# Running decay sums as rows: one broadcast transfer per head in place of four turns on TensorE

## The chip, the cores and the metric

The kernel runs on one NeuronCore of a Trainium2 chip. The metric is device time in microseconds for one execution of the whole program. The engines that matter here: TensorE (PE, matmuls and turns by the identity), its weight load (PEld), VectorE (DVE), ScalarE (ACT), GpSimd (POOL) and SyncE (SP), which issues the DMAs.

## The reference, cut to what matters

Two layers of a hybrid block (a gated delta rule over 8 heads, sliding-window attention, gates, an MLP), then one block with a state-space branch and a pooling branch. Sequence 512, model width 1024, everything in float32. The change touches the delta rule alone, in both layers. There, per head:

```python
g = jnp.cumsum(g, axis=-1)                       # running sum of the log decay, within a chunk
diff = g[..., :, None] - g[..., None, :]
decay = jnp.where(causal, jnp.exp(jnp.where(causal, diff, 0.0)), 0.0)
L = jnp.where(strict, jnp.einsum('bhnid,bhnjd->bhnij', kb, k) * decay, 0.0)
a_intra = jnp.einsum('bhnid,bhnjd->bhnij', q, k) * decay
q_dec = q * jnp.exp(g)[..., None]
```

The kernel works with chunks of 128 positions (4 per head), not 64. It needs the running sums `g` twice: as a column (one number per partition) and as a row (the same 128 numbers of a chunk on every partition), because `diff` has one index on the partitions and one along them, and because `q` is stored with its channels on the partitions, so that `exp(g)` must stand as a row to scale it.

## The kernel before, in words

**Products.** Activations are stored turned, channels on partitions, as [128, 8, 512]. Each weight tile of 512 KB is loaded into one of three buffers `raw` by SP (`load_weights`, lines 882 to 886, which waits until the tile three before it has been split), split into a high part by ScalarE (line 899) and a low part by GpSimd (line 906), and used in 24 matmuls of 128x512 (`products`, lines 933 to 935: high by high, high by low, low by high). An output tile is scaled out of PSUM by VectorE (line 1693).

**The order.** Every engine runs a written list. A planner, `ordered` (line 277), takes chains of stages, the needs between chains, the engine of each stage and its cost in microseconds, and always places the stage that can start first; `layer_order` (line 407) gives it the chains of one layer, and each engine's function walks through the result and does the stages that are its own. SP's list is made of weight loads (and some transfers of the third block); it waits in order like any other. Within a chain, a stage waits for a semaphore that counts the finished stages of the chain (`G.before`, `D.before`).

**The gates, chain G** (once per layer). TensorE turns the gates' projection, VectorE and ScalarE make the log decay `gg` (128 positions by 4 chunks by 8 heads), and stage "cumsum" multiplies it on TensorE by a triangle of ones and by ones (lines 1819 and 1820), into bank 0 of `psD`. "copyc" (line 1500, VectorE) copies the sums to `gcl`; "diff", "exps" and "nbeg" make three exponentials and a negation from them.

**The heads, chain D** (8 per layer). Stages in order: square, sums, qscale, turnk, ksum, root, copyk, turnv, recip, dscale, copyv, rows, diff, exps, qdec, gramk, maskk, first, minus, gramq, maskq. All that TensorE makes here goes to bank 0 of `psD`, one stage after the other. The stages near the change are these:
- "rows" (line 1834, TensorE): for each of the 4 chunks it takes the column of sums of this head, repeated along 128 columns, and turns it, so that the sums stand as a row on all partitions.
- "diff" (line 1522, VectorE): 4 instructions, rows minus column, then the minimum with a mask; the result goes to `DT`.
- "exps" (lines 1348 and 1349, ScalarE): the exponential of the rows, from PSUM into `rna` (which is the buffer `rstdp`; the trace calls it so), and that of `DT` in place.
- "qdec" (line 1272, GpSimd): q times `rna`.

After D a head goes through chain A (the inverse of the triangular matrix, many small matmuls and masks) and chain B (the scan over chunks), while the planner mixes the weight products of later tiles in between.

Of the kernel before, what the change touches and what calls it, by code (L numbers as in the profile page):

```python
# [14 lines left out]
P = 128  # L15
# [174 lines left out]
def e_stages(tile):  # L190
# [3 lines left out]
    if kind == "f2":  # L194
# [7 lines left out]
            "cumsum", "copyc", "diff", "exps", "nbeg"]  # L202

D_STAGES = ["square", "sums", "qscale", "turnk", "ksum", "root", "copyk", "turnv", "recip", "dscale", "copyv", "rows", "diff", "exps",
# [30 lines left out]
N_STAGES = ["highs", "adds"]  # L235
R_STAGES = ["cast", "angle"] + [f"{s}{i}" for s in "sc" for i in range(6)] + ["sin", "sign"]
# [85 lines left out]
for _engine, _kind, _stages in [  # L322
        ("pe", "G", "turn cumsum"), ("act", "G", "tanh abs expn ln expa exps"),
        ("pe", "D", "sums rows gramk gramq turnk turnv"), ("act", "D", "square ksum root exps copyk copyv"), ("pool", "D", "qdec"),
        ("pe", "A", "p q turn plast qlast"), ("act", "A", "copy copylast"),
        ("pe", "B", "v o r kv turno"), ("act", "B", "copyv osq square root high"), ("pool", "B", "low"),
        ("pe", "C", "score turn pv"), ("act", "C", "exp copy high"),
        ("pe", "E", "dupk turnv"), ("act", "E", "tap3 tanh copyk copyv high square"), ("pool", "E", "low"),
        ("act", "N", "highs"), ("vector", "N", "adds"), ("act", "R", "sin"), ("act", "M", "square high"), ("pool", "M", "low"),
        ("act", "Z", "dt mag sines kcopy"), ("pe", "Z", "kmm"), ("dma", "Z", " ".join(Z_DMA)),  # L330
        ("sp", "SU", "uout uin"), ("dma", "SU", "ulanded landed"), ("sp", "SY", "yout yin"), ("dma", "SY", "ylanded landed"),
        ("act", "SY", "gelu high"), ("pe", "S", "input output"), ("act", "S", "copyy"),
        ("act", "BA", "high"), ("pool", "BA", "low")]:
    for _s in _stages.split():
        LAYER_ENGINES[_kind, _s] = _engine


def micros(e):

    kind, j, s = e  # L340
    if kind == "mm":
        return 5.12 / PARTS
    if kind == "split_high":
        return 1.1
    if kind == "split_low":
# [8 lines left out]
    special = {("N", "highs"): 2.5, ("N", "adds"): 3.0, ("A", "update"): 0.45, ("A", "turn"): 0.6, ("A", "p"): 1.1, ("A", "q"): 1.1, ("A", "plast"): 0.6, ("A", "qlast"): 0.6,  # L354
# [16 lines left out]
    return special.get((kind, name), LENGTH[engine_of(e)])  # L371
# [35 lines left out]
def layer_order(layer):  # L407
# [11 lines left out]
    def needs(e):  # L419
# [64 lines left out]
        if kind == "Z" and s == "dt":  # L484
            out.append(e_last(("f1", KT - 1)))
        if kind == "G" and s == "turn":
            out.append(e_last(("ab", 0)))
        if kind == "D":
            if s == "square":
                out.append(e_last(("v", j)))  # L490
            if s == "copyk" and TAKEN[j] is not None:
                out.append(("B", TAKEN[j], "o"))
            if s == "rows" and j == 0:
                out.append(last("G", 0))
            if s == "maskk" and j >= 3:
                out.append(last("A", GROUP_OF[j - 3]))
# [19 lines left out]
    chains += [[("C", t, s) for t in range(o, SWQ, 2) for s in C_STAGES] for o in range(2)]  # L516
    chains.insert(0, [("N", i, s) for i in range(2) for s in N_STAGES])
# [150 lines left out]
def build(nc, xT, pos, consts, gain0, params, weights, params2, smallbc, uD, yD, matsD, lagsD, outT):  # L668

    with ExitStack() as ctx:  # L670
# [3 lines left out]
        def sem(name):  # L674
            return ctx.enter_context(nc.semaphore(name))
# [63 lines left out]
        ab = U1  # L739
        rna = rstdp  # L740
# [168 lines left out]
        def part(layer, earlier):  # L909
            names = ("tile_stage", "gate_stage", "gram_stage", "inverse_stage", "scan_even", "scan_odd", "window_even", "window_odd", "mlp_even", "mlp_odd",  # L910
                     "coef_stage", "x_ready", "sq_done", "h_high", "h_low", "ssq_done", "root_done", "rstd_ready", "x_scaled", "post_col", "pre_col", "pre_row",
                     "pre_sum", "sq_added", "post_sum", "coef_in", "sum_done", "post_root", "post_ready", "out_done", "setup", "out_ready", "state_stage", "y_stage",
                     "branch_even", "branch_odd", "mats_out", "mats_even", "mats_odd", "u_out", "u_even", "u_odd", "y_out", "y_in")
# [3 lines left out]
             branch_even, branch_odd, mats_out, mats_even, mats_odd, u_out, u_even, u_odd, y_out, y_in) = [sem(f"{n}{layer}") for n in names]  # L917
# [336 lines left out]
            if layer < DEPTH:  # L1254
                def run_sync(sp):
                    if layer == 0:
                        start_sync(sp)
                    for kind, j, s in L_ORDERS[layer]:
                        if kind == "load":
                            load_weights(sp, NL * layer + j)  # L1260
                        elif kind == "Z" and s.rstrip("0123") in Z_DMA:
                            coefficient_transfers(sp, s)

# [30 lines left out]
                def run_scalar(act):  # L1294
                    for kind, j, s in L_ORDERS[layer]:
# [37 lines left out]
                        elif kind == "D" and s in ("square", "ksum", "root", "exps", "copyk", "copyv"):  # L1333
# [13 lines left out]
                            elif s == "exps":  # L1347
                                act.activation(rna[:, :], psD[:, 0, :], ACT.Exp)
# [121 lines left out]
                def run_vector(v):  # L1470
                    for kind, j, s in L_ORDERS[layer]:
# [5 lines left out]
                        elif kind == "G":  # L1477
                            if s not in ("copy", "beta", "addb", "max", "plus1", "sp", "g", "copyc", "diff", "nbeg"):
                                continue
# [19 lines left out]
                            elif s == "copyc":  # L1499
                                ins = v.tensor_copy(gcl, psD[:, 0, 0:64])  # L1500
                            elif s == "diff":
# [4 lines left out]
                        elif kind == "D" and s in ("qscale", "recip", "dscale", "diff", "maskk", "maskq", "first", "minus"):  # L1506
# [233 lines left out]
                def run_tensor(pe):  # L1740
# [3 lines left out]
                    for kind, j, s in L_ORDERS[layer]:  # L1744
# [65 lines left out]
                        elif kind == "G" and s in ("turn", "cumsum"):  # L1810
# [5 lines left out]
                            else:  # L1816
# [3 lines left out]
                                ins = pe.matmul(psD[:, 0, 32:64], k_("ones"), gg, start=True, stop=True)  # L1820
                            ins.then_inc(gate_stage, 1)
                        elif kind == "D" and s in ("sums", "rows", "gramk", "gramq", "turnk", "turnv"):
# [3 lines left out]
                            if s == "rows" and h == 0:  # L1826
                                pe.wait_ge(gate_stage, G.end(0))
                            for c in range(CH):
                                i, cc = c * HEADS + h, slice(c * P, (c + 1) * P)
# [552 lines left out]
```

## Time and profile before

| | us |
|---|---|
| median of 3 runs | 2522.82 (2521.14 to 2523.16) |
| the profiled execution | 2522.34 |
| its span in the trace | 2520.6 |
| TensorE busy | 2421.3 (96%) |
| VectorE busy | 1256.3 (50%) |
| GpSimd busy | 1153.6 (46%) |
| ScalarE busy | 1057.5 (42%) |

Numbers of the sections ahead and below come from the profiled execution. "Busy" of TensorE counts the time in which at least one matmul is under way. Matmuls overlap: each of 128x512 is shown with some 390 ns, while they start 230 ns apart, so what a group of them takes is read from the starts, not from the durations. `L1834` is line 1834 of the kernel.

### The profile page before, as it was taken

The page shows a single profiled execution, that of the slowest core. Times are in us where ns is not written, and L with a number is a line of the kernel's source. Part 1 is how long each engine was busy: PE and PEld are TensorE (multiplying, and loading weights), DVE is VectorE, ACT ScalarE, POOL GpSimd, SP SyncE. Part 2 cuts the span into 40 slices and gives each one's busy share as a digit, 9 for nine tenths or more (in the row PEclk, how much of TensorE's full clock was granted, in tenths as well). Part 3 has the DMA queues.
Part 4 walks back from the last instruction along what each step waited for, and adds up shares of the span by engine and source line. Part 5 has one row for each costly group of instructions (what it writes and reads, how often), then busy time and mean ns, then how long its engine had stood idle before and what let it go on. Part 6 is the DMA issues. An engine that isn't in the chain of part 4 may idle for free.

```text
span 2520.6 us, 35035 instructions
## 1 busy us (share of the span) xinstructions
PE 2421.3 (96%) x13972; PEld 1924.9 (76%) x13972; DVE 1256.3 (50%) x2172; ACT 1057.5 (42%) x2254; POOL 1153.6 (46%) x848
## 2 busy tenths in 40 slices
PE   7999999999999999988999999999999999799998
PEld 5777777777778888766878777787777788677886
DVE  4767654673341111266667446633485511566453
ACT  5565643543343323345566434443533332313342
POOL 4323323334666555543323233356665564433464
PEclk9999999999999999989999999999999999878999
DMA  4211112122223233311111122223234332362232
GB/s 138 67 51 51 51 43 68 59 76 76 92 76 100 92 94 99 101 59 51 58 44 60 43 68 67 68 84 110 66 111 122 121 98 93 99 185 85 93 99 75
DMA packets 76514, 207.47 MB, mean 82 GB/s; under 512 B 16704, under 2 KB 27712, under 8 KB 75840
## 3 DMA queue, kind: packets, MB, share of 16 engines
q1 hardware_dynamic: 76352, 205.24, 25.9%
q8 instruction: 110, 1.80, 0.3%
q14 instruction: 52, 0.43, 0.1%
HBM read 194.72 MB, written 10.49 MB: 81 GB/s over the span
## 4 chain that ended last, share of the span: by engine, by line
PE 81%; DVE 9%; ACT 4%; POOL 2%; issue 2%; DMA 1%; SPq 0%; DVEq 0%; ACTq 0%; POOLq 0%
PE ps L933 23%; PE ps L935 21%; PE ps L934 21%; PE ps L1855 2%; PE ps L1859 2%; PE ps L1908 1%; PE ps L1920 1%; PE ps L1836 1%; POOL wL L906 1%; ACT wH L899 1%; PE ps L1914 1%; ACT prob L1404 1%; DVE ctw L1143 1%; DVE ctmp L1143 1%; PE ps L1885 1%
## 5 line engine op out<-in xcount | busy, mean ns | idle before, releaser
L906 POOL TENSOR_TENSOR wL<-raw,wH 128x512 fp32r<-128x512 f32 x660 | 901.7, 1388 | 1143.7 <-ACT wH L899 1143.4
L899 ACT ACTIVATE wH<-raw 128x512 fp32r<-128x512 f32 x660 | 379.7, 624 | 769.5 <-PE ps L935 766.1
L933 PE MATMUL ps<-hH,wH 128*128 128x512 f32 x1592 | 667.5, 419 | 11.0 <-DVE tmp L1693 8.8
L935 PE MATMUL ps<-hH,wL 128*128 128x512 f32 x1592 | 633.4, 398 | 0.0
L934 PE MATMUL ps<-hL,wH 128*128 128x512 f32 x1592 | 631.2, 396 | 0.0
L933 PEld LDWEIGHTS ps<-hH,wH 128*128 128x128 f32 x1592 | 303.7, 191 | 82.8 <-issue 22.7
L935 PEld LDWEIGHTS ps<-hH,wL 128*128 128x128 f32 x1592 | 303.4, 191 | 67.8
L934 PEld LDWEIGHTS ps<-hL,wH 128*128 128x128 f32 x1592 | 304.9, 191 | 54.9 <-issue 0.7
L933 PE MATMUL ps<-OH,wH 128*128 128x512 f32 x576 | 230.8, 401 | 4.9 <-DVE acc L1722 1.8
L935 PE MATMUL ps<-OH,wL 128*128 128x512 f32 x576 | 227.8, 396 | 0.0
L934 PE MATMUL ps<-OL,wH 128*128 128x512 f32 x576 | 227.8, 395 | 0.0
L933 PE MATMUL ps<-SH,wH 128*128 128x512 f32 x436 | 172.6, 396 | 0.0
L935 PE MATMUL ps<-SH,wL 128*128 128x512 f32 x436 | 172.5, 396 | 0.0
L934 PE MATMUL ps<-SL,wH 128*128 128x512 f32 x436 | 172.4, 395 | 0.0
L933 PEld LDWEIGHTS ps<-OH,wH 128*128 128x128 f32 x576 | 108.2, 188 | 36.7 <-issue 9.2
L1724 DVE TENSOR_TENSOR acc<-acc,ps 128x512 f32<-128x512 f32 x48 | 33.0, 687 | 202.0 <-PE ps L935 202.0
L935 PEld LDWEIGHTS ps<-OH,wL 128*128 128x128 f32 x576 | 108.2, 188 | 26.1
L934 PEld LDWEIGHTS ps<-OL,wH 128*128 128x128 f32 x576 | 108.3, 188 | 24.8
L933 PEld LDWEIGHTS ps<-SH,wH 128*128 128x128 f32 x436 | 81.9, 188 | 20.2 <-issue 0.4
L934 PEld LDWEIGHTS ps<-SL,wH 128*128 128x128 f32 x436 | 81.9, 188 | 19.8
L935 PEld LDWEIGHTS ps<-SH,wL 128*128 128x128 f32 x436 | 81.9, 188 | 19.7
L1404 ACT ACTIVATE prob<-prob,small 128x256 f32<-128x256 f32 (+1 forms) x128 | 59.9, 469 | 61.6 <-DVE small L1640 61.6
(405 smaller groups left out, 3461.8 us busy)
## 6 DMA issues: line engine op xcount, KB each, us to landing
raw<-w SPq DMA_DIRECT2D x345, 512.0 KB, 3.5
mats<-matsD SPq DMA_DIRECT2D x4, 1408.0 KB, 6.6
x<-xT SPq DMA_DIRECT2D x8, 256.0 KB, 5.8
matsD<-Cd SPq DMA_DIRECT2D x8, 256.0 KB, 2.7
matsD<-wide SPq DMA_DIRECT2D x4, 512.0 KB, 3.6
mats<-lagsD SPq DMA_DIRECT2D x32, 64.0 KB, 6.4
outT<-acc SPq DMA_DIRECT2D x8, 256.0 KB, 2.2
matsD<-tab SPq DMA_DIRECT2D x8, 128.0 KB, 1.9
```

The lines of the kernel that those rows point to most:

```text
L899: act.activation(weights_at(slot)[0][:, k, :], raw[:, n % RAW, k, :], ACT.Copy).then_inc(high_done, 1)
L906: pool.tensor_tensor(low[:, k, :], raw[:, n % RAW, k, :], high[:, k, :].bitcast(F32), ALU.subtract).then_inc(low_done, 1)
L933: pe.matmul(out, wh, rH[:, t, :], start=(t == 0), stop=False)
L934: pe.matmul(out, wh, rL[:, t, :], start=False, stop=False)
L935: mm = pe.matmul(out, wl, rH[:, t, :], start=False, stop=(t == depth - 1))
L1143: return v.tensor_tensor(o, a, b, ALU.mult)
L1404: act.activation(prob[:, i, a:], prob[:, i, a:], ACT.Exp, bias=nm4[:, i:i + 1], accum_out=den[:, i:i + 1])
L1724: ins = v.tensor_tensor(acc[:, i % 8, :], acc[:, i % 8, :], b, ALU.add)
L1836: ins = pe.matmul(psD[:, 0, cc], k[:, cc], (k if s == "gramk" else q)[:, cc], start=True, stop=True)
L1855: ins = pe.matmul(psA[b, 0, cc], lt[b, c, b], Xi[b, i, :], start=True, stop=True)
L1859: ins = pe.matmul(second_half(psA[b, 0, cc], n), Pm[b, i, :], second_half(xb[b, i, :], n), start=True, stop=True)
L1885: ins = pe.matmul(psS[e], XT[SLOT[h]][:, c, :], vb[SLOT[h]][:, 0, :] if c == 0 else rr, start=True, stop=True)
```

## The change

The 4 turns of each head go. In their place the gates' chain computes the sums once more in turned form, with `gg` as the weights and the triangle as the moving operand: 32 partitions (chunk and head) by 128 positions. A new stage "copyr" copies them to SBUF (`gclT`, 32 x 128, in a tile of the scan that is not yet in use). SP writes them to DRAM in 4 transfers, one per chunk, so that each head's 512 sums lie in one row of `yD` (a DRAM tensor of the third block). For each head SP reads that row with a broadcast over 128 partitions into `rna`. "diff" takes its rows from `rna`, and "exps" works in place there. The reads and writes are a new chain "GR" for the planner (its stages "outlanded" and "landed" stand for the landing of a transfer). The first "sums" now waits for "copyr", and the wait for the end of the gates moves from "rows" of head 0 on TensorE to "diff" of head 0 on VectorE. Semaphores that a block does not use are no longer made.

```diff
 G_STAGES = [...
-            "cumsum", "copyc", "diff", "exps", "nbeg"]
+            "cumsum", "copyc", "copyr", "diff", "exps", "nbeg"]
-D_STAGES = [..., "dscale", "copyv", "rows", "diff", "exps",
+D_STAGES = [..., "dscale", "copyv", "diff", "exps",
...
+ROWS = [(-1, "out"), (-1, "outlanded")] + [(h, s) for h in range(HEADS) for s in ("in", "landed")]
...
# the planner's costs, in its microseconds
+    special = {("GR", "out"): 1.2, ("GR", "in"): 0.4, ("GR", "outlanded"): 3.0, ("GR", "landed"): 3.5, ...
-               ("D", "rows"): 0.45,
...
# the planner's needs
+        if kind == "GR" and s == "out":
+            out.append(("G", 0, "copyr"))
+        if kind == "GR" and s == "in" and j:
+            out.append(("D", j - 1, "qdec"))
...
+            if (j, s) == (0, "sums"):
+                out.append(("G", 0, "copyr"))
+            if (j, s) == (0, "copyk"):
+                out.append(("G", 0, "exps"))
-            if s == "rows" and j == 0:
-                out.append(last("G", 0))
+            if s == "diff":
+                out.append(("GR", j, "landed"))
+                if j == 0:
+                    out.append(last("G", 0))
...
+        gclT = osqs[0][0:CH * HEADS, 0:P]
...
# SP
+                        elif kind == "GR" and s == "out":
+                            sp.wait_ge(gate_stage, G.before(0, "copyr") + 1)
+                            for c in range(CH):
+                                sp.dma_start(yD[layer, 0:HEADS, c * P:(c + 1) * P], gclT[c * HEADS:(c + 1) * HEADS, :]).then_inc(rows_out, 16)
+                        elif kind == "GR" and s == "in":
+                            if j == 0:
+                                sp.wait_ge(rows_out, 16 * CH)
+                            else:
+                                sp.wait_ge(gram_stage, D.before(j - 1, "qdec") + 1)
+                            sp.dma_start(rna[:, :], yD[layer, j:j + 1, :].to_broadcast([P, SEQ])).then_inc(rows_in, 16)
...
# ScalarE, "exps"
-                                act.activation(rna[:, :], psD[:, 0, :], ACT.Exp)
+                                act.activation(rna[:, :], rna[:, :], ACT.Exp)
...
# VectorE
+                            elif s == "copyr":
+                                ins = v.tensor_copy(gclT, psD[0:CH * HEADS, 0, P:2 * P])
...
                             elif s == "diff":
+                                v.wait_ge(rows_in, 16 * (h + 1))
+                                if h == 0:
+                                    v.wait_ge(gate_stage, G.end(0))
                                 for c in range(CH):
                                     i = c * HEADS + h
-                                    ins = v.scalar_tensor_tensor(out=DT[:, c, :], in0=a0[:, c, :], scalar=gcl[:, i:i + 1],
+                                    ins = v.scalar_tensor_tensor(out=DT[:, c, :], in0=chunks(rna[:, :])[:, c, :], scalar=gcl[:, i:i + 1],
                                                                  in1=k_("later"), op0=ALU.subtract, op1=ALU.min)
...
# TensorE
-                                ins = pe.matmul(psD[:, 0, 32:64], k_("ones"), gg, start=True, stop=True)
+                                pe.matmul(psD[:, 0, 32:64], k_("ones"), gg, start=True, stop=True)
+                                ins = pe.matmul(psD[0:CH * HEADS, 0, P:2 * P], gg, k_("upper"), start=True, stop=True)
...
-                            if s == "rows" and h == 0:
-                                pe.wait_ge(gate_stage, G.end(0))
+                            if s == "sums" and h == 0:
+                                pe.wait_ge(gate_stage, G.before(0, "copyr") + 1)
...
-                                elif s == "rows":
-
-                                    ins = pe.transpose(psD[:, 0, cc], gcl[:, i:i + 1].to_broadcast([P, P]), ident)
```

## Rows read from the trace of the kernel before

**Rows 1.** The page, busy time, share of the span and instructions of each engine.

```profile
PE 2421.3 (96%) x13972; PEld 1924.9 (76%) x13972; DVE 1256.3 (50%) x2172; ACT 1057.5 (42%) x2254; POOL 1153.6 (46%) x848
```

**Rows 2.** The page, the chain of waits by engine.

```profile
PE 81%; DVE 9%; ACT 4%; POOL 2%; issue 2%; DMA 1%; SPq 0%; DVEq 0%; ACTq 0%; POOLq 0%
```

**Rows 3.** Windows: stretch, length, busy us of each engine, granted clock, DMA share, GB/s.

```profile
60.00:100.00 40.00, 34.43 (x191) 27.45 (x190) 34.49 (x59) 23.11 (x47) 17.43 (x12) 0.98 0.25 76
100.00:350.00 250.00, 245.15 (x2116) 193.94 (x2115) 166.46 (x352) 147.27 (x354) 79.40 (x57) 0.99 0.16 50
1120.00:1200.00 80.00, 71.79 (x480) 55.80 (x478) 52.25 (x92) 39.57 (x88) 28.02 (x20) 0.98 0.19 60
1200.00:1410.00 210.00, 208.85 (x1841) 166.86 (x1839) 139.43 (x306) 128.38 (x312) 66.83 (x50) 1.00 0.16 51
```

**Rows 4.** Waits of TensorE, 1095 to 1200 us: total, times, longest.

```profile
PE ps L933 <- DVE tmp L1693: 5.7, 4, 2.8
```

**Rows 5.** Line 1834: ns shortest, median, longest; first and last start.

```profile
L1834 PE MATMUL ps<-cst,small x64: 270/273/323, 83.1 to 1406.2; 128*128 128x128 f32 x64
```

**Rows 6.** Timeline, TensorE at three heads: start, length, [idle before <- releaser].

```profile
83.10 0.65 PE L1834 MATMUL ps<-cst,small 128*128 128x128 f32 x4 [0.56 <-ACT vb L1358]
83.50 0.48 PE L933 MATMUL ps<-hH,wH 128*128 128x512 f32 x1
...
150.62 0.60 PE L1834 MATMUL ps<-cst,small 128*128 128x128 f32 x4
150.98 0.47 PE L933 MATMUL ps<-hH,wH 128*128 128x512 f32 x1
151.29 0.39 PE L934 MATMUL ps<-hL,wH 128*128 128x512 f32 x1
151.52 0.39 PE L935 MATMUL ps<-hH,wL 128*128 128x512 f32 x1
...
1149.11 0.65 PE L1834 MATMUL ps<-cst,small 128*128 128x128 f32 x4 [0.56 <-ACT vb L1358]
```

**Rows 7.** Timeline, the gates' sums of layer 1.

```profile
1113.99 0.41 PE L1819 MATMUL ps<-small,cst 128*128 128x32 f32 x2 [3.62 <-DVE small L1496]
...
1114.45 0.48 PE L933 MATMUL ps<-hH,wH 128*128 128x512 f32 x1
...
1114.65 0.23 DVE L1500 COPY small<-ps 128x64 f32<-128x64 f32 x1 [0.72 <-PE ps L1820]
```

**Rows 8.** DMA issues with KB and us to landing; one issue in the timeline.

```profile
raw<-w SPq DMA_DIRECT2D x345, 512.0 KB, 3.5
...
yD<-Y SPq DMA_DIRECT2D x4, 256.0 KB, 3.2
...
kr<-pos SPq DMA_DIRECT2D x1, 256.0 KB, 6.4
...
12.91 0.43 SPq L1053 DMA_DIRECT2D kr<-pos  x1
```

**Rows 9.** Timeline: "qdec" of head 0, then "diff" of head 1, layer 0.

```profile
86.88 1.29 POOL L1272 TENSOR_TENSOR qd<-qs,rstdp 128x512 f32<-128x512 f32 x1 [5.93 <-ACT DT L1349]
...
116.52 1.12 DVE L1522 SCALAR_TENSOR_TENSOR DT<-ps,small,cst 128x128 f32<-128x128 f32 x4 [0.28 <-PE ps L1834]
```

**Rows 10.** Waits of SP, 60 to 420 us; two weight splits three tiles apart.

```profile
SPq L886 <- POOL wL L906: 355.6, 36, 16.9
...
117.28 1.16 ACT L899 ACTIVATE wH<-raw 128x512 fp32r<-128x512 f32 x2 [2.85 <-PE ps L935]
...
149.19 1.15 ACT L899 ACTIVATE wH<-raw 128x512 fp32r<-128x512 f32 x2 [0.64 <-PE ps L935]
```

**Rows 11.** Lines 1522 and 1696, ns shortest, median, longest; middle tap: busy, mean ns.

```profile
L1522 DVE SCALAR_TENSOR_TENSOR DT<-ps,small,cst x64: 339/342/352, 84.5 to 1407.3; 128x128 f32<-128x128 f32 x64
...
L1696 DVE SCALAR_TENSOR_TENSOR vs<-tmp,par,vs x48: 704/745/1671, 61.6 to 1385.9; 128x511 f32<-128x511 f32 x16, 128x510 f32<-128x510 f32 x16, 128x509 f32<-128x509 f32 x16
...
L1696 DVE SCALAR_TENSOR_TENSOR vs<-tmp,par,vs 128x510 f32<-128x510 f32 x16 | 15.9, 991 | 0.2
```

More of the change, by code:

```diff
@@ L201 @@
 G_STAGES = ["turn", "copy", "tanh", "beta", "addb", "max", "abs", "expn", "plus1", "ln", "sp", "expa", "g",
-            "cumsum", "copyc", "diff", "exps", "nbeg"]
-D_STAGES = ["square", "sums", "qscale", "turnk", "ksum", "root", "copyk", "turnv", "recip", "dscale", "copyv", "rows", "diff", "exps",
+            "cumsum", "copyc", "copyr", "diff", "exps", "nbeg"]
+D_STAGES = ["square", "sums", "qscale", "turnk", "ksum", "root", "copyk", "turnv", "recip", "dscale", "copyv", "diff", "exps",
             "qdec", "gramk", "maskk", "first", "minus", "gramq", "maskq"]
@@ L323 @@
         ("pe", "G", "turn cumsum"), ("act", "G", "tanh abs expn ln expa exps"),
-        ("pe", "D", "sums rows gramk gramq turnk turnv"), ("act", "D", "square ksum root exps copyk copyv"), ("pool", "D", "qdec"),
+        ("pe", "D", "sums gramk gramq turnk turnv"), ("act", "D", "square ksum root exps copyk copyv"), ("pool", "D", "qdec"),
         ("pe", "A", "p q turn plast qlast"), ("act", "A", "copy copylast"),
@@ L330 @@
         ("act", "Z", "dt mag sines kcopy"), ("pe", "Z", "kmm"), ("dma", "Z", " ".join(Z_DMA)),
-        ("sp", "SU", "uout uin"), ("dma", "SU", "ulanded landed"), ("sp", "SY", "yout yin"), ("dma", "SY", "ylanded landed"),
+        ("sp", "GR", "out in"), ("dma", "GR", "outlanded landed"), ("sp", "SU", "uout uin"), ("dma", "SU", "ulanded landed"), ("sp", "SY", "yout yin"), ("dma", "SY", "ylanded landed"),
         ("act", "SY", "gelu high"), ("pe", "S", "input output"), ("act", "S", "copyy"),
@@ L353, in micros @@
         return (0.5, 1.2, 2.4, 3.0, 4.8, 3.6, 7.2)[int(s[len(name):])]
-    special = {("N", "highs"): 2.5, ("N", "adds"): 3.0, ("A", "update"): 0.45, ("A", "turn"): 0.6, ("A", "p"): 1.1, ("A", "q"): 1.1, ("A", "plast"): 0.6, ("A", "qlast"): 0.6,
+    special = {("GR", "out"): 1.2, ("GR", "in"): 0.4, ("GR", "outlanded"): 3.0, ("GR", "landed"): 3.5, ("N", "highs"): 2.5, ("N", "adds"): 3.0, ("A", "update"): 0.45, ("A", "turn"): 0.6, ("A", "p"): 1.1, ("A", "q"): 1.1, ("A", "plast"): 0.6, ("A", "qlast"): 0.6,
                ("A", "copy"): 2.0, ("A", "copylast"): 0.6, ("A", "negate"): 0.6,
@@ L516, in layer_order @@
     chains += [[("C", t, s) for t in range(o, SWQ, 2) for s in C_STAGES] for o in range(2)]
+    chains.append([("GR", h, s) for h, s in ROWS])
     chains.insert(0, [("N", i, s) for i in range(2) for s in N_STAGES])
@@ L909, in part @@
         def part(layer, earlier):
+            FIRST_BLOCK = ("gate_stage", "key_stage", "gram_stage", "inverse_stage", "scan_even", "scan_odd", "window_even", "window_odd", "mlp_even",
+                           "mlp_odd", "coef_stage", "coef_in", "setup", "mats_out", "rows_out", "rows_in")
+            SECOND_BLOCK = ("out_done", "out_ready", "state_stage", "y_stage", "branch_even", "branch_odd", "mats_even", "mats_odd", "u_out",
+                            "u_even", "u_odd", "y_out", "y_in")
             names = ("tile_stage", "gate_stage", "gram_stage", "inverse_stage", "scan_even", "scan_odd", "window_even", "window_odd", "mlp_even", "mlp_odd",
@@ L912, in part @@
                      "pre_sum", "sq_added", "post_sum", "coef_in", "sum_done", "post_root", "post_ready", "out_done", "setup", "out_ready", "state_stage", "y_stage",
-                     "branch_even", "branch_odd", "mats_out", "mats_even", "mats_odd", "u_out", "u_even", "u_odd", "y_out", "y_in")
+                     "branch_even", "branch_odd", "mats_out", "mats_even", "mats_odd", "u_out", "u_even", "u_odd", "y_out", "y_in", "rows_out", "rows_in")
             (tile_stage, gate_stage, gram_stage, inverse_stage, scan_even, scan_odd, window_even, window_odd, mlp_even, mlp_odd,
@@ L916, in part @@
              pre_sum, sq_added, post_sum, coef_in, sum_done, post_root, post_ready, out_done, setup, out_ready, state_stage, y_stage,
-             branch_even, branch_odd, mats_out, mats_even, mats_odd, u_out, u_even, u_odd, y_out, y_in) = [sem(f"{n}{layer}") for n in names]
+             branch_even, branch_odd, mats_out, mats_even, mats_odd, u_out, u_even, u_odd, y_out, y_in, rows_out, rows_in) = [sem(f"{n}{layer}") if n not in (FIRST_BLOCK if layer == DEPTH else SECOND_BLOCK) else None for n in names]
             window_stage = (window_even, window_odd)
@@ L1477, in run_vector @@
                         elif kind == "G":
-                            if s not in ("copy", "beta", "addb", "max", "plus1", "sp", "g", "copyc", "diff", "nbeg"):
+                            if s not in ("copy", "beta", "addb", "max", "plus1", "sp", "g", "copyc", "copyr", "diff", "nbeg"):
                                 continue
@@ L1819, in run_tensor @@
                                 pe.matmul(psD[:, 0, 0:32], k_("upper"), gg, start=True, stop=True)
-                                ins = pe.matmul(psD[:, 0, 32:64], k_("ones"), gg, start=True, stop=True)
+                                pe.matmul(psD[:, 0, 32:64], k_("ones"), gg, start=True, stop=True)
+                                ins = pe.matmul(psD[0:CH * HEADS, 0, P:2 * P], gg, k_("upper"), start=True, stop=True)
                             ins.then_inc(gate_stage, 1)
-                        elif kind == "D" and s in ("sums", "rows", "gramk", "gramq", "turnk", "turnv"):
+                        elif kind == "D" and s in ("sums", "gramk", "gramq", "turnk", "turnv"):
                             h = j
@@ L1825, in run_tensor @@
                             q, k, vv = qs[h % 2][:, :], ks[h % 4][:, :], vs[h % 2][:, :]
-                            if s == "rows" and h == 0:
-                                pe.wait_ge(gate_stage, G.end(0))
+                            if s == "sums" and h == 0:
+                                pe.wait_ge(gate_stage, G.before(0, "copyr") + 1)
                             for c in range(CH):
-                                i, cc = c * HEADS + h, slice(c * P, (c + 1) * P)
+                                cc = slice(c * P, (c + 1) * P)
                                 if s == "sums":
                                     ins = pe.matmul(psD[:, 0, c:c + 1], sq[:, 1, cc], k_("ones")[:, 0:1], start=True, stop=True)
-                                elif s == "rows":
-                                    ins = pe.transpose(psD[:, 0, cc], gcl[:, i:i + 1].to_broadcast([P, P]), ident)
                                 elif s in ("gramk", "gramq"):
```

2 rows, old and new, of the table special are left out of this document.

## The prediction

> **What bounds the kernel now.** I read the page's busy times first: TensorE is busy 2421.3 of 2520.6 us, and no other engine passes 1256.3 [rows 1]. The chain of waits agrees, with 81% of the span on TensorE and 1% on DMA [rows 2]. Then the two places where the change works, cut into windows: layer 0's heads run from about 60 to 350 us and layer 1's from about 1120 to 1410 us. In the stretches 100 to 350 and 1200 to 1410 TensorE is busy 245.15 of 250.00 and 208.85 of 210.00 us at a granted clock of 0.99 and 1.00 (the higher level, 2.4 GHz); while the first heads of each layer pass, it is busy only 34.43 of 40.00 and 71.79 of 80.00 [rows 3]. So its idle time in all four is 5.57 + 4.85 + 8.21 + 1.15 = 19.8 us. The table of waits says who ends it: at the start of layer 1 the largest cause is VectorE's scaling of a projected tile, 5.7 us [rows 4]. What the reader is to see: with the heads in flight the time is the sum of what TensorE is given to do, and a piece of work taken off it comes back in full; at the first head of each layer VectorE sets the pace, and there it may not.
>
> **The four turns.** Stage "rows" is 64 transposes (2 layers, 8 heads, 4 chunks), median 273 ns each [rows 5]. 64 x 0.273 = 17.5 us would be wrong, because a matmul starts long before the one ahead of it has ended. What counts is the distance from the first start of the group to the start of what follows: 0.40 us (83.10 to 83.50) and 0.36 us (150.62 to 150.98) [rows 6]. Over the 16 groups 0.36 to 0.41 gives 5.8 to 6.6 us; I take 6.2. The product matmul after such a group starts its successor 0.31 us later, not 0.23 [rows 6]; that 0.08 goes as well only where the group has products on both sides, and otherwise stays with the small work beside it: 0.2 us in all, bounds 0 and 16 x 0.08 = 1.3. Ahead of the group at the first head of each layer TensorE stood idle 0.56 us for the copy of v [rows 6]. With the group gone that wait goes, 1.1 us for both layers, but at just these heads VectorE is late, so I count it as doubtful.
>
> **What TensorE gets instead.** One more matmul per layer in stage "cumsum". The two that stand there, four entries in the trace, take 0.46 us from 1113.99 to 1114.45, so some 0.23 each for 32 columns [rows 7]. The new one turns 128 columns: 0.23 to 0.40 (a group of four 128-column transposes, [rows 6]); I take 0.25, so 0.5 us for both. It runs while VectorE's chain sets the pace (3.62 us of waiting ahead of it, [rows 7]), so it may also cost nothing.
>
> **The copy "copyr".** VectorE takes 0.23 us for "copyc", 64 columns out of the same bank [rows 7]; 0.2 to 0.4 for 128, twice. Queued behind it are "diff" of the gates, then the taps of q. The first "sums" and the first "copyk" now wait for it or for the gate's exponentials in the plan; "copyc" runs at 1114.65 [rows 7] and head 0's "rows" at 1149.11 [rows 6], and between the first "sums" and "rows" lie less than 15 us of that head's own stages, so some 20 us are left. Cost 0; if the cover were gone, 0.8.
>
> **The way through DRAM.** Per layer four small writes (16 KB together), then eight reads that put 2 KB on each of 128 partitions (256 KB each). The nearest row is the load of the positions, the same shape of broadcast, which landed 6.4 us after its issue in the crowded opening; a 256 KB write to the same DRAM tensor took 3.2 us, and a weight load of 512 KB 3.5 us [rows 8]. I take 3.5 us per read, bounds 2 and 6.4 (no row shows anything under 2). For head 0 of layer 1: sums copied at about 1115.1, four issues of 0.43 us each [rows 8], landed by 1120 (1123 with the longer price), read landed by 1124 to 1130. It is wanted by "diff", which follows the rows at 1149.11 [rows 6]: 19 us in hand. For a later head the read waits until GpSimd's "qdec" of the head before has used the tile: head 0's runs 86.88 to 88.17 and head 1's "diff" starts at 116.52 [rows 9], a gap of 28 us for some 4 to 7. Cost 0. If the cover were gone, each head would lose what is late, on VectorE, with TensorE behind it.
>
> **SP's queue.** It now holds "in" and "out" between weight loads, in the planned order, and a load behind an unready row transfer waits. Before, SP waited 355.6 us for GpSimd over 36 loads in 60 to 420 us [rows 10], so its own 24 issues of 0.43 us (10 us in all) cost nothing. For the loads behind: the splits of one tile start at 117.28 and of the third after it at 149.19 [rows 10]. The load of that third tile may go when the first is split, some 3 us on (two halves on ScalarE, then GpSimd), and takes 3.5 us; it has 31.9 - 3 - 3.5 = 25 us to spare. The wait for the writes (3 to 6 us), or a "qdec" that comes a few us later than planned, is covered. The 16 reads move 4.2 MB beside 207 MB at a DMA share of 0.16 to 0.25 in these windows [rows 3]: 0.
>
> **"diff" and "exps".** "diff" reads the rows from SBUF in place of PSUM, and it takes over two waits: the transfer, and for head 0 the end of the gates. Behind it on VectorE stand taps, scalings and the inverse's masks; both waits are over long before. It no longer waits for TensorE (0.28 us in the row at 116.52, [rows 9]), so a head's chain is shorter by the group and two handovers, about 1 us of 34. This helps only where that chain is late. ScalarE's exponential reads SBUF, not PSUM, at the same size; what it feeds is "qdec", with the 28 us of air above, so I cost it at 0 either way.
>
> **A rule that speaks against the change.** The four "diff" instructions read one operand from PSUM now and never vary, 339 to 352 ns [rows 11]. The taps of v, which read two tensors from SBUF, have a median of 745 ns but reach 1671, and the mean of the middle tap is 991 [rows 11]. The Trainium skill (SBUF — State Buffer, Who interferes with whom) says that a VectorE instruction with two SBUF inputs and a GpSimd instruction that reads SBUF lock each other out for a whole instruction. After the change "diff" has two SBUF inputs, and by that rule it could be held. The trace agrees in that only such rows spread. The result it gives is rival 3.
>
> **The sum.** Profiled execution 2522.3 us (span 2520.6 and 1.7 around it). Groups -6.2, transition -0.2, idle -1.1, new matmuls +0.5: -7.0 if all comes back. If the first head of each layer gives nothing back, 2 x 0.39 + 1.1 = 1.9 less: -5.1. I take -6: 2516.3 us. The median of the runs shown is 2522.82, 0.5 above the profiled time, so this is 0.26% under it. From no change I can tell apart about 0.2%, that is 5.0 us: 2517.8 and below is faster, above 2527.9 slower.
>
> **The written order.** All queues are written out by a planner that gets new stages, costs and needs, so many instructions that the change does not name will move. No row prices this. From below, nothing beyond the 19.8 us of idle time can be won in these stretches. From above, the two layers are two orders for nearly the same work and left 10.4 and 9.4 us idle, so orders differ by single microseconds; but each new gap of the kind at VectorE's scaling (5.7 us in one place, [rows 4]) adds directly. I take 0 and keep -6 and +8 for the range.
>
> **The rivals.**
> 1. Less comes back (2518 to 2524, I would write 2520). The transposes fill moments in which TensorE would wait for VectorE or ScalarE anyway. For it: the idle time at the first heads, and the fact that "busy" is modelled, so that gaps of some 0.1 us between small and large matmuls don't show. Against it: 1.15 us idle in 210.
> 2. More comes back (2509 to 2513): the shorter chain of each head and the new order also close part of the 19.8 us. For it: the chain's two handovers; against it: waits of TensorE on this chain are short.
> 3. Slower, by the lock on VectorE. The place is "diff" of each head, four instructions side by side with GpSimd's split of weights or "qdec". The price of one meeting is the rest of a GpSimd instruction, at most 1.29 us [rows 9], and for the taps of v the middle one's mean of 0.991 us against the median of 0.745 [rows 11] gives 0.25 us per instruction; an instruction of 0.34 us meets less, so 0.15 to 0.25. 64 x 0.15 = 9.6 us, 64 x 0.25 = 16 us of VectorE. It decides only if VectorE has no air left: it is busy 166.46 of 250.00 and 139.43 of 210.00 us [rows 3], so a third is free. With all of it on the path the time is 2516.3 + 9.6 to 16 = 2526 to 2532; 2529 as one number. By the page's rule alone the delay exists, and this air says it is hidden.
> 4. SP's queue blocks the weights: a read of rows queued ahead of a load whose "qdec" comes more than 25 us later. Nothing in the rows comes near; were it so at every head, 14 x 5 us would give about 2590. That the change doesn't do what it says is no case: the 64 transposes leave the code.
>
> **How the numbers follow.** Forecast (2513.5 to 2518.5) 0.47; rival 1 0.22; rival 2 0.10; rival 3 together with new gaps from the order, 2524 to 2532, 0.19; rival 4 0.02. Faster: most of the forecast (0.40) and rival 2, with 0.02 of the order's luck, 0.52. Within 0.2%: 0.07 of the forecast, rival 1, and a small share of rival 3, 0.31. Slower: 0.17. The range to 8 in 10: 2509 to 2526, which takes in rivals 1 and 2 and the mild end of 3; the likeliest case alone is 2513.5 to 2518.5.
>
> **What would show it.** Right: no transposes of the sums, TensorE's busy time down by about 6 us, idle time in the head windows still near 20, SP's reads landing over 15 us before "diff". Wrong: "diff" ended by a DMA; SP waiting for "qdec" and ScalarE's split then waiting for weights; "diff" with a spread of durations and VectorE over nine tenths busy beside a longer span; or TensorE's idle time in these stretches up by as much as the groups gave.

## The result, and the profile after

| | median, us | ratio to before (95% interval) |
|---|---|---|
| before (12 runs, same chip) | 2522.81 | |
| after (12 runs) | 2530.16 | 1.0026 (1.0014 to 1.0037) |

The change made the kernel 0.26% slower, 7.4 us of medians; 2516.3 was predicted, with 2526 as the upper end. One run of after took 2970.72 us with nothing changed in the program; it is left out of the ratio.

The page of after: its span, then busy us (share of the span) and instructions of each engine, then the chain of waits by engine.

```profile
span 2528.5 us, 34957 instructions
PE 2422.2 (96%) x13912; PEld 1923.2 (76%) x13912; DVE 1263.4 (50%) x2174; ACT 1058.1 (42%) x2254; POOL 1152.2 (46%) x848
...
PE 83%; DVE 8%; ACT 4%; POOL 2%; issue 2%; DMA 1%; SPq 0%; DVEq 0%; ACTq 0%; POOLq 0%
```

TensorE has 60 rows fewer, yet is busy 0.9 us longer [rows 1], where 5.9 less was forecast (groups and transition less the new matmuls); its idle time went from 99.3 to 106.3 us (span less busy). So two things were lost besides what the turns gave: 7.0 us of idle time, and 6.8 us of busy time. The size of the second fits the clock: added up inside the span from the trace's record of the granted clock, after runs 128.8 us at the lower level (1.2 GHz) and before 115.1, and half of the 13.7 us more is 6.8. With the forecast's -5.9 that makes +7.9, which is the difference of the spans (2528.5 less 2520.6). This splits two single executions. Their clocks are those of the means over all runs (0.975 and 0.977), but single runs of before range from 0.973 to 0.981.

The stretches of [rows 3] in after (columns as there), and behind them two short ones.

```profile
60.00:100.00 40.00, 35.62 (x189) 28.32 (x188) 34.81 (x58) 22.95 (x47) 16.79 (x12) 0.95 0.25 74
100.00:350.00 250.00, 242.94 (x2055) 191.73 (x2055) 163.06 (x345) 145.62 (x349) 81.57 (x59) 0.98 0.18 58
1120.00:1200.00 80.00, 70.48 (x459) 54.91 (x458) 51.29 (x94) 39.56 (x90) 26.78 (x20) 0.96 0.20 63
1200.00:1410.00 210.00, 207.00 (x1779) 164.43 (x1779) 144.67 (x301) 124.28 (x302) 69.82 (x51) 0.99 0.19 58
...
285.00:305.00 20.00, 16.58 (x107) 12.96 (x106) 7.24 (x15) 11.31 (x28) 3.87 (x3) 0.83 0.15 52
1195.00:1215.00 20.00, 18.90 (x161) 15.31 (x160) 10.19 (x21) 12.10 (x31) 3.68 (x3) 0.91 0.10 27
```

The idle time of the four is 4.4 + 7.1 + 9.5 + 3.0 = 24.0 us, against 19.8, and the granted clock is lower in each. The short stretch from 285 to 305 us has 3.4 us of it, at a clock of 0.83. The same stretch of before:

```profile
285.00:305.00 20.00, 19.51 (x169) 14.77 (x169) 12.42 (x23) 14.17 (x32) 7.02 (x6) 1.00 0.16 54
```

What TensorE waited for in after from 60 to 450 us (total, times, longest), its first rows:

```profile
PE ps L1866 <- POOL qd L1299: 3.6, 3, 1.4
PE ps L1864 <- ACT sq L1365: 2.9, 1, 2.9
PE ps L1868 <- ACT kd L1382: 1.9, 1, 1.9
PE ps L1889 <- DVE Pm L1587: 1.1, 2, 0.5
```

And of before, where "sums" (line 1831) waits less for ScalarE's square and gramk (line 1836) less for GpSimd's "qdec":

```profile
PE ps L933 <- DVE tmp L1693: 2.6, 4, 1.3
PE ps L1859 <- DVE Pm L1555: 2.0, 2, 1.4
PE ps L1838 <- ACT kd L1355: 1.9, 1, 1.9
PE ps L1831 <- ACT sq L1338: 1.5, 1, 1.5
...
PE ps L1836 <- POOL qd L1272: 0.5, 1, 0.5
```

None of after's rows in this window is a DMA, and none is the new path: they are old stages that now meet each other badly. The timeline of after shows the two largest, first "gramk" behind "qdec", then "sums" behind the square:

```profile
120.58 1.71 POOL L1299 TENSOR_TENSOR qd<-qs,rstdp 128x512 f32<-128x512 f32 x1
...
122.31 0.33 SPq L1289 DMA_DIRECT2D rstdp<-yD  x1
...
122.34 1.16 PE L1866 MATMUL ps<-ks 128*128 128x128 f32 x8 [1.40 <-POOL qd L1299]
...
289.75 1.28 ACT L1459 ACT_TABLE_LOAD   x1
291.04 0.63 ACT L1459 ACTIVATE tmp<-vs 128x512 f32<-128x512 f32 x1
...
292.49 0.63 ACT L1365 ACTIVATE sq<-qs 128x512 f32<-128x512 f32 x1 [0.82 <-DVE vs L1731]
...
293.17 1.00 PE L1864 MATMUL ps<-cst,sq 128*128 128x1 f32 x6 [2.90 <-ACT sq L1365]
```

In the second, TensorE's list has the head's "sums" at a point where ScalarE has just come to the head's activation and square; TensorE can do nothing else meanwhile, because its list is fixed. It stood idle 0.53 and then 2.90 us before its clock fell to the lower level, for 6.8 us from 294 to 301. Before's list has one such wait in the whole window, 1.5 us long, and none in this stretch.

The new parts themselves behave: lines of after for the DMAs (KB, us to landing) and, by itself, the range of the 16 reads; SP's waits in the whole run; and "diff" (shortest, median, longest; then busy, mean ns):

```profile
rstdp<-yD SPq DMA_DIRECT2D x16, 256.0 KB, 3.3
...
DMA to landing us min/median/max: 3.0/3.3/3.8
...
SPq L1289 <- POOL qd L1299: 48.4, 14, 11.2
...
SPq L1283 <- DVE osq L1529: 9.7, 2, 6.4
...
L1554 DVE SCALAR_TENSOR_TENSOR DT<-rstdp,small,cst x64: 310/345/1359, 83.7 to 1419.3; 128x128 f32<-128x128 f32 x64
...
L1554 DVE SCALAR_TENSOR_TENSOR DT<-rstdp,small,cst 128x128 f32<-128x128 f32 x64 | 20.1, 374 | 1.1 <-ACT vb L1385 1.1
...
87.44 0.33 SPq L1289 DMA_DIRECT2D rstdp<-yD  x1
...
113.73 1.14 DVE L1554 SCALAR_TENSOR_TENSOR DT<-rstdp,small,cst 128x128 f32<-128x128 f32 x4 [0.23 <-ACT vb L1385]
```

The read of head 1, issued at 87.44, lands by 91 us, 23 us before its "diff".

### The profile page after: what moved, and what is told of

It reads as the page before. It is cut to its first block, busy times and chain, and to the rows that moved or that the text cites. A ratio compares the mean times of both kernels' runs of the same rounds, so it can differ in the third digit from the quotient of the medians.

```text
span 2528.5 us, 34957 instructions
## 1 busy us (share of the span) xinstructions
PE 2422.2 (96%) x13912; PEld 1923.2 (76%) x13912; DVE 1263.4 (50%) x2174; ACT 1058.1 (42%) x2254; POOL 1152.2 (46%) x848
## 4 chain that ended last, share of the span: by engine, by line
PE 83%; DVE 8%; ACT 4%; POOL 2%; issue 2%; DMA 1%; SPq 0%; DVEq 0%; ACTq 0%; POOLq 0%
PE ps L950 23%; PE ps L952 22%; PE ps L951 22%; PE ps L1885 2%; PE ps L1889 2%; PE ps L1938 1%; PE ps L1866 1%; PE ps L1950 1%; ACT wH L912 1%; POOL wL L919 1%; DVE ctw L1160 1%; PE ps L1944 1%; ACT prob L1431 1%; DVE ctmp L1160 1%; PE ps L1915 1%
## 5 line engine op out<-in xcount | busy, mean ns | idle before, releaser
L951 PEld LDWEIGHTS ps<-SL,wH 128*128 128x128 f32 x436 | 81.9, 188 | 19.6
```

What stands on the lines that cost most here:

```text
L951: pe.matmul(out, wh, rL[:, t, :], start=False, stop=False)
```

## The experiments

The expectations of the first four name three theories. A: the order that the planner writes once "rows" is gone costs what the turns gave, and more. B: the new parts cost it directly (two SBUF inputs, transfers, SP's queue). C: the turns were free for TensorE, and the order alone is paid. "In place" means that the planner still plans the list of before and the change is put into the finished list. Each run stands against before on the same chip; I name differences under 0.2% only with their intervals. "At full clock" is the mean over the runs of span times granted clock (standard error 0.4 to 0.7 us), which takes the clock's part out by arithmetic; before has 2462.4, after 2463.9.

**e1: the whole change, the order of before.**

```diff
+def in_place(plan):      # strike "rows"; "copyr" behind "copyc"; GR "out" behind it,
+                         # GR 0 "in" behind the next load, GR h+1 "in" behind "qdec" of h
-    return ordered(chains, needs, engine_of, slack1, .2)
+    return in_place(ordered(chains, needs, engine_of, slack1, .2))
```

> The whole change, but every engine keeps the written order of the kernel before: the planner plans the old stages, then 'rows' is struck from the list, 'copyr' stands behind 'copyc', the writes behind 'copyr', the first read behind the next weight load, and each later read behind the 'qdec' of the head before. Theory A (the new written order costs what the turns gave, and more): about 6 us below before, 0.25%. Theory B (the mechanism itself costs: VectorE's 'diff' with two SBUF inputs against GpSimd, or SP's queue): as the changed kernel, 6 to 8 us above before. Theory C (the turns were free for TensorE, and the order is what is paid): within 2 us of before.

Measured: 2521.50, ratio 0.9989 (0.9978 to 1.0000), about -2.8 us. That is half of what A asks (-6), just outside C (within 2 us), and far from B (+6 to +8).

**e2: nothing of the change but its order**: the planner gets the new chains and needs, the turns are put back into the list ahead of "diff".

```diff
+def with_rows(plan):     # strike GR and "copyr"; ("D", h, "rows") ahead of ("D", h, "diff")
-    return ordered(chains, needs, engine_of, slack1, .2)
+    return with_rows(ordered(chains, needs, engine_of, slack1, .2))
```

> The kernel before with its four turns and no transfer of rows, but with the written order that the planner makes for the changed kernel; 'rows' stands just ahead of 'diff'. Theory A: 6 us or more above the changed kernel's time less 6, that is some 10 to 14 us above before. Theory B: within 3 us of before. Theory C: 6 to 8 us above before, as the changed kernel.

Measured: 2532.95, ratio 1.0041 (1.0028 to 1.0053), 10.3 us more, as A has it (10 to 14), and 7.4 us more at full clock. The same instructions as before in another order cost more than the change did, and the change in before's order costs nothing: the slowdown is the order's. The four kernels close a square. Put into the order of before, the change gives -0.11% (e1); put into the order of after, it gives -0.15% (after against e2, 1.0026 and 1.0041). One stretch shows it in three kernels (columns as above): e2, with the turns and after's order, has after's gap to the hundredth and after's clock; e1, with the transfers and before's order, has neither.

```profile
285.00:305.00 20.00, 16.58 (x106) 12.87 (x105) 7.27 (x15) 10.88 (x27) 3.87 (x3) 0.83 0.18 53
```

```profile
285.00:305.00 20.00, 19.52 (x147) 14.90 (x147) 12.88 (x25) 13.04 (x31) 6.34 (x5) 1.00 0.16 53
```

**e3: order of before, the rows left out** (neither turns nor transfers, so the decay isn't computed), and **e4: each turn twice.**

```diff
# e3
+    return [e for e in ordered(...) if e[0] != "D" or e[2] != "rows"]
# e4
+                                    pe.transpose(psD[:, 0, cc], gcl[:, i:i + 1].to_broadcast([P, P]), ident)
                                     ins = pe.transpose(psD[:, 0, cc], gcl[:, i:i + 1].to_broadcast([P, P]), ident)
```

> The kernel before in its own order, with stage 'rows' left out and nothing in its place: 'diff' and 'exps' then work on what v's turns left in the bank, so the decay is not computed. It bounds what taking the turns away can give with no price for anything else. By the sum of the prediction: -6 us (-5 to -7). Theory C: within 1 us of before.

> The kernel before in its own order with every turn of the sums made twice, 64 transposes more. If a group costs its 0.35 to 0.41 us of TensorE also when it is added: +6 us (5 to 8). Theory C: within 1 us of before.

Measured: e3 2515.98, ratio 0.9975 (0.9962 to 0.9987), which is -6.3 us; e4 2531.92, ratio 1.0036 (1.0026 to 1.0047), +9.1 us where 5 to 8 was expected. Both rule out C. The turns do cost what their starts say (6.2 us), or more where a second group is pushed in. The timeline of e1, TensorE at the place of [rows 6], has the products 0.24 us behind the small matmul ahead of them, with no group between:

```profile
151.70 0.49 PE L1929 MATMUL ps<-rr,XT 128*128 128x128 f32 x2
151.94 0.48 PE L964 MATMUL ps<-hH,wH 128*128 128x512 f32 x1
```

**e5: e1 without its transfers** (the rows keep old contents, the exponential runs with scale 0, so the decay isn't computed), and **e6: before with "diff" reading SBUF** (old contents, the turns stay).

```diff
# e5: GR "out", GR "in" and the wait for rows_in go
-                                act.activation(rna[:, :], rna[:, :], ACT.Exp)
+                                act.activation(rna[:, :], rna[:, :], ACT.Exp, scale=0.0)
# e6
-    in0=a0[:, c, :]
+    in0=chunks(rna[:, :])[:, c, :]
```

> The change in the old order (as e1_old_order), but SP writes and reads no rows and VectorE waits for none; 'diff' works on what is in the tile, and the exponential of the rows is taken with a scale of 0, so the decay is not computed. The third matmul of the gates, 'copyr' and the two SBUF inputs of 'diff' stay. e1_old_order stood 2.8 us below before and e3_no_rows 6.3. If SP's queue or the transfers cost the 3.5 between them: -6. If VectorE's 'diff' from SBUF against GpSimd does: -3, as e1_old_order.

> The kernel before, order and turns kept, with one edit: 'diff' takes its rows operand from SBUF (the rows of the head before, so DT is wrong) and not from PSUM. The price of the lock between VectorE and GpSimd by itself. If that is what ate the rest in e1_old_order: +3 us. If not: within 1 us of before.

Measured: e5 2525.37, ratio 1.0007 (0.9994 to 1.0021); e6 2523.40, ratio 1.0005 (0.9990 to 1.0019). Neither price that was expected of e5 came (-6 or -3). Without transfers the kernel isn't faster than e1; at full clock it is 0.9 us less, within the error, but its granted clock was lower (0.9749 against e1's 0.9767), and nothing here says why. By the full clock transfers cost 0.9 us, and with the error at most some 2.4. e6 gives +1.3 us, between its two expectations. In e6 "diff" (shortest, median, longest; busy, mean ns) spreads as in after:

```profile
L1522 DVE SCALAR_TENSOR_TENSOR DT<-rstdp,small,cst x64: 337/346/1358, 84.5 to 1409.2; 128x128 f32<-128x128 f32 x64
...
L1522 DVE SCALAR_TENSOR_TENSOR DT<-rstdp,small,cst 128x128 f32<-128x128 f32 x64 | 21.9, 403 | 6.6 <-PE ps L1834 6.3
```

Before it never left 339 to 352 ns [rows 11]. One input moved from PSUM to SBUF brings the spread, and the traces show with whom the long ones meet. At one place before and e6 both have "diff" beside GpSimd's split of weights; before's four instructions take 1.12 us together, e6's 2.12, because the first of them takes 1337 ns and ends just after the split does. First before, then e6:

```profile
149.90 2.55 POOL L906 TENSOR_TENSOR wL<-raw,wH 128x512 fp32r<-128x512 f32 x2 [11.71 <-ACT wH L899]
151.26 1.12 DVE L1522 SCALAR_TENSOR_TENSOR DT<-ps,small,cst 128x128 f32<-128x128 f32 x4 [0.56 <-PE ps L1834]
```

```profile
149.85 2.56 POOL L906 TENSOR_TENSOR wL<-raw,wH 128x512 fp32r<-128x512 f32 x2 [11.71 <-ACT wH L899]
151.23 2.12 DVE L1522 SCALAR_TENSOR_TENSOR DT<-rstdp,small,cst 128x128 f32<-128x128 f32 x4 [0.56 <-PE ps L1834]
```

In before 13 of the 64 "diff" instructions overlap a GpSimd instruction and none is longer than 352 ns. In e6 5 overlap one and 4 of these take over 1000 ns; in after 4 overlap one and take 566 to 1359 ns. The Trainium skill (SBUF — State Buffer, Who interferes with whom) states that a VectorE instruction with two SBUF inputs contends with a GpSimd instruction that reads SBUF; the traces agree, with these durations. But 64 x (403 - 343), the mean of e6 less that of before, is 3.8 us of VectorE (2.0 in after), and TensorE hardly sees it.

**e7 and e8: before, only the planner's price of "rows" altered.** The instructions are those of before. Is after's order bad for what is in it, or is it one draw among many?

```diff
-               ("D", "rows"): 0.45,
+               ("D", "rows"): 0.30,      # e7; 0.60 in e8
```

> The kernel before with nothing changed but a number of the planner: the cost of 'rows' is 0.30 in place of 0.45. Every instruction stays; 224 and 155 of TensorE's stages in the two layers change places. If any new order of this planner costs what the changed kernel's did: +6 to +10 us. If the changed kernel's order is an unlucky one: anywhere within 3 us of before.

> As e7_cost_030, with the cost of 'rows' at 0.60: 176 and 225 stages of TensorE change places. The same two expectations. If this and e7_cost_030 differ from each other by more than 3 us, the order is a lottery rather than a steady price.

Measured: e7 2526.23, ratio 1.0019 (1.0006 to 1.0032), between its two expectations; e8 2519.48, ratio 0.9989 (0.9975 to 1.0002). A price that alters no instruction, only their order, moves the time by 6.7 us of medians between the two, over the 3 us that was set as the sign of a lottery.

**e9: the change in place (as e1) in e8's order**, and **e10: after once more.**

```diff
# e9, on e1
-               ("D", "rows"): 0.45,
+               ("D", "rows"): 0.60,
```

> The change, put in place as in e1_old_order, but into the order of e8_cost_060 (the planner's cost of the struck stage 'rows' is 0.60). If the price of an order and the gain of the change are separate terms, they add: -2.8 (e8_cost_060) -2.8 (e1_old_order) = -5.6 us, 0.22%. If the order is a lottery for each kernel anew, also where the list of all other stages is the same, anywhere from -6 to +5.

> The changed kernel itself once more, on the same chip as the others of this call. If its share of reduced clock (mean 0.9748 against 0.9769) belongs to the kernel: again +6 to +7 us and 0.975. If it was the luck of those runs: +1.5 us and 0.977.

Measured: e9 2517.92, ratio 0.9982 (0.9972 to 0.9992); e10 2528.78, ratio 1.0022 (1.0013 to 1.0032), so after's loss repeats, and so does its clock (0.9748). e9 came to -4.5 us, near the -5.6 of two terms that add. It contains the whole change and beats both kernels. The same stretches of e9: no gap, full clock.

```profile
285.00:305.00 20.00, 20.00 (x169) 15.81 (x168) 11.98 (x25) 15.00 (x36) 6.50 (x6) 1.00 0.16 54
...
1195.00:1215.00 20.00, 20.00 (x182) 16.18 (x181) 15.93 (x33) 13.58 (x37) 6.75 (x5) 1.00 0.09 28
```

**e11 and e12: after, with one other number in the planner.** "diff" priced at its measured 1.12 us (four instructions in [rows 9]) in place of 1.4, and the handover between engines at 0.25 in place of 0.2.

```diff
-               ("D", "diff"): 1.4,
+               ("D", "diff"): 1.12,      # e11
-    return ordered(chains, needs, engine_of, slack1, .2)
+    return ordered(chains, needs, engine_of, slack1, .25)      # e12
```

> The changed kernel with one number of its planner changed: the cost of 'diff' 1.12 in place of 1.4 (172 and 288 of TensorE's stages change places). If transfers or VectorE's lock were what makes the changed kernel slower: +6 us, as it. If it is the one order: nearer to e1_old_order, between -3 and +4.

> The changed kernel with the planner's handover at 0.25 in place of 0.2 (240 and 297 of TensorE's stages change places). The same two expectations as e11_diff_112: +6 if the mechanism is what costs, -3 to +4 if it is the one order.

Measured: e11 2518.17, ratio 0.9978 (0.9966 to 0.9990); e12 2527.76, ratio 1.0015 (1.0005 to 1.0025). After and e11 run the same instructions and lie 0.4% apart on the same chip (e10 and e11). e11 is better than its range (-3 to +4) and speaks for the order; e12, at +3.8 us, lies inside that range but its interval reaches +6, so by itself it decides nothing.

All kernels together. Idle is TensorE's in the four stretches of [rows 3], from the windows of one profile each; the clock is the mean granted one over the runs. The idle time doesn't rank the kernels by itself: e3 is the fastest with 22.8 us.

| kernel | turns | order | ratio | full clock, us | clock | idle, us |
|---|---|---|---|---|---|---|
| before | yes | before | 1 | 2462.4 | .9769 | 19.8 |
| e8 | yes | rows at 0.60 | 0.9989 | 2459.9 | .9770 | 16.9 |
| e2 | yes | after | 1.0041 | 2469.8 | .9760 | 23.7 |
| e7 | yes | rows at 0.30 | 1.0019 | 2463.7 | .9757 | 19.6 |
| e6 | yes, unused | before | 1.0005 | 2463.7 | .9769 | 19.1 |
| e4 | twice | before | 1.0036 | 2470.3 | .9763 | 18.6 |
| e3 | left out | before | 0.9975 | 2456.8 | .9768 | 22.8 |
| e5 | no | before | 1.0007 | 2458.9 | .9749 | 22.5 |
| e1 | no | before | 0.9989 | 2459.8 | .9767 | 22.5 |
| e9 | no | rows at 0.60 | 0.9982 | 2458.7 | .9768 | 18.3 |
| e11 | no | diff at 1.12 | 0.9978 | 2457.9 | .9768 | 19.5 |
| e12 | no | handover at 0.25 | 1.0015 | 2464.8 | .9759 | 21.8 |
| after | no | after | 1.0026 | 2463.9 | .9748 | 24.0 |
| e10 | no | after | 1.0022 | 2463.6 | .9748 | 25.5 |

## Why the prediction was wrong, by its steps

**The step that failed is "The written order": "I take 0".** With the order held, the change gives -0.11% (e1); with its own order it gives +0.26%. The difference, 0.37% or about 9 us, is the order; e2 measures it by itself at +0.41%, 10.3 us. The text kept +8 for the range, but counted it in a case of 0.19 and not in the centre, and ended the range at 2526. It also looked only for gaps, and its sum has no term for the clock: after against e1 is 4.1 us at full clock, and the rest is clock (0.9748 against 0.9767, each 0.001 being 2.5 us of span). That the order alone costs this clock is not shown. e2 has after's order and 0.9760, and e5 has before's order and 0.9749.

What in the change makes the order? I compared the lists that the planner writes. Adding chain GR and its needs while keeping "rows" moves none of TensorE's stages. The lists of e1 are before's and those of e2 are after's, stage for stage, on all four compute engines. Striking the 0.45 us stage "rows" from chain D moves 189 of TensorE's 1469 stages in layer 0 and 235 of 1473 in layer 1, and 128 and 185 of VectorE's. The planner always takes the stage that can start first by its own costs, so a shift of 0.45 us settles many near ties the other way, all down the layer.

**The four turns: right.** -6.2 was forecast, e3 gave -6.3 (-9.6 to -3.3); e4's +9.1 puts no smaller price on them. That the centre fits so well is in part luck, for the interval is 6 us wide. Part of the gain did become waiting, as rival 1 said: with the order held, the idle time in the four stretches rose by 2.7 (e1) and 3.0 us (e3).

**New matmuls, copy, transfers, "diff": too small.** +0.5 was forecast for all; e1 less e3 is 0.14%, 3.5 us of ratio and 3.0 at full clock, where the error is some 1.7. The transfers are 0.9 of it (e5) and the operand in SBUF 1.3 (e6), each with an error as large; 0.5 for the matmuls is the forecast's and was not measured alone. These add up to 2.7, but none of the small terms is resolved alone.

**The way through DRAM and SP's queue: right.** Reads land in 3.0 to 3.8 us (3.5 taken), 23 us before "diff" for head 1 and at least 18 us for any of the 16; SP waits 48.4 us for "qdec" in 14 waits of its reads, the longest 11.2, and ScalarE's splits wait no longer for weights: 3.0 us in the whole run, against 3.1 before.

**Rival 3** named the right side and its second half, the gaps of a new order, for the wrong main reason. The lock exists and costs VectorE 2.0 us where 9.6 to 16 was priced: 60 of after's 64 "diff" instructions meet no GpSimd instruction, and the median is 345 ns. The price was put on each of the 64, as if every one had a neighbour. Of the 2 to 4 us of VectorE little reaches the time (e6: +1.3 us, -2.5 to +4.8 by its ratio). The prediction's remark that only rows with two SBUF inputs spread is too wide as well: before's line 1639 reads one tensor and goes from 158 to 1236 ns.

**Of what would show it**, the sign named last came in part: TensorE's idle time in these stretches rose by 4.2 us (24.0 less 19.8), not by the 6.2 of the groups; only over the whole span is it more, 7.0. "Diff" spreads, but VectorE is busy for half of the span and not for nine tenths. The signs for lateness of a DMA or of weights did not come. What I had not listed was busy time that rises at fewer instructions.

**What stays open.** Which activity makes the clock fall. In after it fell behind waits of 0.53 and 2.90 us. But with the turns gone and before's order kept (e1, e3) it also fell near 173 us, for 6.8 and 3.4 us, where TensorE is as busy as in before:

```profile
165.00:185.00 20.00, 19.50 (x137) 14.84 (x136) 11.49 (x21) 12.52 (x30) 3.55 (x3) 0.83 0.16 53
```

(e1; before has 19.50 us busy there too, at 1.00.) And e6, with before's order, has 0.91 between 285 and 305 us with 19.51 us busy, where before has 1.00. Nor is it known why e5 has a lower clock than e1, of which it is a copy without the transfers and with old contents in the tile. Why e1 gives 3 us less than e3 is open too. The clock is not the reason, for the difference stands at full clock, and both have the same rise in idle time. Also open is whether e11's and e9's orders are good or lucky: I read their idle time after the runs, and no number of the planner foretold it.

## What to carry to other kernels

When every queue is written out by a planner, an edit of 6 us comes with a new order, and here the order alone moved the time from -0.1% (e8) to +0.4% (e2). Before judging such an edit, run it in the old order; then try a few planner costs for both versions and compare best with best: e9 and e11 (0.18% and 0.22% faster than before) keep the change, and before's own best order tried here, e8, gave 0.11%. The gain of the change itself is then some 0.1% (0.11% with before's order, 0.15% with after's, 0.07% with e8's, 0.11% best with best, these last two between runs on two chips). By the time none of these alone is clear of its interval; at full clock the first two are (2.6 and 5.9 us).

Count busy time at its clock: if fewer instructions give the same busy time, look at the granted clock before looking for slower instructions.

## What the runs showed that I had not expected

- The mean granted clock repeats for one and the same kernel and differs between kernels of the same instructions: after has 0.9748 in both studies (e10), while e1, e9 and e11 have 0.9767 to 0.9768. The order isn't all that sets it: e5, with e1's order and no transfers, has 0.9749.
- A broadcast of one 2 KB row of DRAM to 128 partitions lands in 3.0 to 3.8 us, half of the 6.4 us of the same shape in the crowded opening [rows 8], and its issue takes 0.33 us.
- One operand moved from PSUM to SBUF took a VectorE instruction that never varied (339 to 352 ns) to a longest of 1358 ns, with the median nearly unmoved (346 against 342).
